# Two mixers' ends by token tiles, latent columns as 352 and 352, and a state product moved ahead of a level

## The reference

```python
def second_block(x, ...):
    for l in range(2):
        h = _rmsnorm(x, mix_norm[l])
        c_q, c_kv, k_pe, hq, hf, hi, hg = jnp.split(h @ w_in[l], splits, axis=-1)   # 384, 256, 64, 4 x 512
        a = _mla(c_q, c_kv, k_pe, positions, ...)            # 4 heads, causal
        r = _hgrn2(hq, hf, hi, hg, lower[l], hg_out_norm[l]) # 4 heads
        x = x + jnp.concatenate([a, r], axis=-1) @ w_out[l]
        x = x + (_swiglu if l == 0 else _moe)(_rmsnorm(x, ffn_norm[l]), ...)
    return _rmsnorm(x, final_norm)

def _mla(...):
    q = (_rmsnorm(c_q, q_a_norm) @ w_q_b)      # per head 128 + 64 columns, the 64 are rotated
    kv = (_rmsnorm(c_kv, kv_a_norm) @ w_kv_b)  # per head 128 of keys, 128 of values
    ...                                        # softmax over the keys up to the query, times v

def _hgrn2(q_raw, f_raw, i_in, g_raw, lower_bound, out_norm):
    q = silu(q_raw); f = lb + (1 - lb) * sigmoid(f_raw)
    log_f = log(f); k = (1 - lb) * sigmoid(-f_raw)
    S_t = diag(f_t) S_{t-1} + (1 - f_t) outer i_t; o_t = S_t^T q_t
    return _rmsnorm(o, out_norm) * silu(g_raw)
```

## Time and profile before

| | us |
|---|---|
| median of 3 runs | 1884.51 |
| lowest and highest | 1883.92, 1885.49 |
| the profiled execution | 1884.52 |
| its span in the profile | 1882.6 |
| PE busy in the span | 1859.7 (99%) |
| DVE busy | 1520.7 (81%) |
| ACT busy | 1240.1 (66%) |
| POOL busy | 402.8 (21%) |

### The profile page before, as it was taken

How to read it: one execution, slowest core, us unless ns; L and a number is a source line. 1 busy time by engine, 2 the same in 40 slices (tenths; PEclk the granted TensorE clock), 3 DMA queues, 4 the chain that set the end, 5 groups by cost and what they waited for, 6 DMA issues and landing times.

```text
span 1882.6 us, 26088 instructions
## 1 busy us (share of the span) xinstructions
PE 1859.7 (99%) x9336; PEld 1563.7 (83%) x9336; DVE 1520.7 (81%) x1650; ACT 1240.1 (66%) x1484; POOL 402.8 (21%) x206
## 2 busy tenths in 40 slices
PE   9999999999999999999999999999999999999997
PEld 7888889888888888878888888888888888888886
DVE  6745357777776887697699999999999999999997
ACT  6654444444754344565588888888888888888876
POOL 6856870002734000371630000000000000000000
PEclk9999999999999999999999999999999999999999
DMA  9534556665444666534699999999999999999994
GB/s 287 169 123 135 179 179 226 223 232 179 132 138 134 218 238 224 163 125 146 221 381 396 391 383 376 388 395 366 388 367 390 395 364 389 366 387 395 371 396 184
DMA packets 251542, 524.20 MB, mean 278 GB/s; under 512 B 9960, under 2 KB 58736, under 8 KB 251328
## 3 DMA queue, kind: packets, MB, share of 16 engines
q1 hardware_dynamic: 243408, 504.00, 74.7%
q10 hardware_dynamic: 5824, 12.06, 1.8%
q0 software_dynamic: 2224, 7.01, 1.2%
HBM read 507.71 MB, written 15.34 MB: 278 GB/s over the span
## 4 chain that ended last, share of the span: by engine, by line
PE 90%; DVE 7%; ACT 1%; issue 1%; DMA 1%; POOL 0%; SPq 0%; DVEq 0%; ACTq 0%
PE bank L740 24%; PE bank L742 24%; PE bank L741 24%; PE bank L1101 6%; PE bank L1104 3%; PE bank L863 1%; PE bank L1368 1%; PE bank L836 1%; DVE arena L1950 1%; DVE arena L2441 1%; DVE arena L1954 1%; PE bank L1182 1%; DMA arena<-in_w_in 1%; DVE arena L2106 1%; PE bank L842 0%
## 5 line engine op out<-in xcount | busy, mean ns | idle before, releaser
L1999 DVE TENSOR_TENSOR w_lo_sb<-arena,w_hi_sb 128x1024 fp32r<-128x1024 f32 x672 | 807.7, 1223 | 74.0 <-ACT w_hi_sb L1522 43.8
L1522 ACT ACTIVATE w_hi_sb<-arena 128x1024 fp32r<-128x1024 f32 x672 | 711.2, 1062 | 168.6 <-PE bank L742 167.9
L740 PE MATMUL bank<-w_hi_sb,left_sb 128*128 128x512 f32 (+1 forms) x1400 | 553.2, 395 | 1.4 <-POOL w_lo_sb L669 1.3
L742 PE MATMUL bank<-w_hi_sb,left_sb 128*128 128x512 f32 (+1 forms) x1400 | 542.2, 387 | 0.0
L741 PE MATMUL bank<-w_lo_sb,left_sb 128*128 128x512 f32 (+1 forms) x1400 | 541.5, 387 | 0.0
L1542 ACT ACTIVATE w_hi_sb<-arena 128x1024 fp32r<-128x1024 f32 (+1 forms) x269 | 278.2, 1051 | 300.8 <-PE bank L742 218.6
L669 POOL TENSOR_TENSOR w_lo_sb<-arena,w_hi_sb 128x1024 fp32r<-128x1024 f32 (+1 forms) x134 | 341.1, 2564 | 536.9 <-ACT w_hi_sb L1542 473.9
L740 PEld LDWEIGHTS bank<-w_hi_sb,left_sb 128*128 128x128 f32 x1400 | 263.1, 188 | 57.9 <-POOL w_lo_sb L669 3.5
L742 PEld LDWEIGHTS bank<-w_hi_sb,left_sb 128*128 128x128 f32 x1400 | 262.9, 188 | 54.9
L741 PEld LDWEIGHTS bank<-w_lo_sb,left_sb 128*128 128x128 f32 x1400 | 263.4, 188 | 50.9 <-issue 0.7
L740 PE MATMUL bank<-w_hi_sb,hid_hi_sb 128*128 128x512 f32 x656 | 257.3, 392 | 0.1
(11 more groups left out here) (365 smaller groups left out, 1676.1 us busy)
## 6 DMA issues: line engine op xcount, KB each, us to landing
arena<-in_moe_w_gate SPq DMA_DIRECT2D x112, 1024.0 KB, 7.6
arena<-in_moe_w_up SPq DMA_DIRECT2D x112, 1024.0 KB, 8.0
arena<-in_moe_w_down SPq DMA_DIRECT2D x112, 1024.0 KB, 7.8
arena<-in_w_in SPq DMA_DIRECT2D x45, 1024.0 KB, 5.1
arena<-in_w_ffn_in SPq DMA_DIRECT2D x22, 1024.0 KB, 5.1
arena<-in_w_out SPq DMA_DIRECT2D x12, 1024.0 KB, 5.0
arena<-in_w_ffn_out SPq DMA_DIRECT2D x11, 1024.0 KB, 4.8
arena<-in_dense_w_gate SPq DMA_DIRECT2D x11, 1024.0 KB, 5.4
```

Source lines behind the costliest of these rows:

```text
L740: pe.matmul(out, still[0], moving[0], start=start, stop=False)
L742: return pe.matmul(out, still[1], moving[0], start=False, stop=stop)
L1522: act.activation(expert_buffer(w_hi_sb, j), expert_piece(j % MOE_SUBS), ACT.Copy) \
L1999: dve.tensor_tensor(expert_buffer(w_lo_sb, j), expert_piece(j % MOE_SUBS), expert_buffer(w_hi_sb, j).bitcast(F32), ALU.subtract) \
```

## The change

It has seven parts.

1. The latents are c0 and c1 of 352 columns each, loaded as two loads of four k tiles each, so that both have four pieces of two k tiles.
2. PE makes level 2 behind the fourth piece of c1 (before: the second of two) and level 3 behind the second piece of hi (before: the first).
3. In layer 1 the logarithm of the bounds' rest is taken earlier on ACT, and DVE makes the keys' logarithm as two sums, of which the first needs the bounds alone.
4. The reciprocal root of the latents' mean squares is ACT's Sqrt and DVE's reciprocal instead of ACT's Ln and Exp; the means (`mean_c`) are taken ahead of level 2.
5. PE makes the state product ahead of level 5, between the two key/value products; DVE copies it right behind its taking of level 4.
6. The mixer's end goes by token tiles: transposes of the weights, products with the values, transposes of the mixed rows and the rounding for tile 0, then for tile 1. The outputs of the linear attention go through the gemm banks and are copied by ACT. `first_mixed` takes the first two weight pieces, tile by tile, and makes the transposes of tile 1 in between.
7. `finish_bounds` is cut into four steps, at units 3 to 6 of f2.

The diff, cut to its core:

```diff
+C_HALF = (Q_RANK + KV_RANK + ROPE) // 2
...
-        add(f"c0_{layer}", w, 0, 512)
-        add(f"c1_{layer}", w, 512, base - 512)
+        add(f"c0_{layer}", w, 0, base // 2)
+        add(f"c1_{layer}", w, base // 2, base // 2)
...
-                 (f"hqT_{layer}", 2), *level[0:4], (f"cT_{layer}", 3), *level[4:6], (f"hst_{layer}", 1),
+                 (f"hqT_{layer}", 2), *level[0:4], (f"cT_{layer}", 3), level[4], (f"hst_{layer}", 1), level[5],
                  (f"mpT_{layer}", 2), level[6], (f"msc0_{layer}", 2),
-                 level[7], (f"msc1_{layer}", 2), (f"ho_{layer}", 2), (f"mP_{layer}", 3), (f"mo_{layer}", 2),
-                 (f"mixT_{layer}", 4),
+                 level[7], (f"msc1_{layer}", 2), (f"mP0_{layer}", 1), (f"mo0_{layer}", 1), (f"mP1_{layer}", 2),
+                 (f"mixA_{layer}", 1), (f"mo1_{layer}", 1), (f"mixB_{layer}", 3),
...
-                gemm(f"c1_{l}", between={1: lambda: level(2)})
-                gemm(f"hi_{l}", between={0: lambda: level(3), 2: turn_c})
+                gemm(f"c1_{l}", between={3: lambda: level(2)})
+                gemm(f"hi_{l}", between={1: lambda: level(3), 2: turn_c})
...
+                for t in range(T):
+                    job = gemm_at[f"wo0_{layer}"] + t
+                    b, tokens = gemm_bank[job % 4][:, :], slice(t * P, (t + 1) * P)
+                    pe.wait_ge(sem("gemm_read"), job - 3)
+                    pe.wait_ge(sem("mix_hi_ready"), layer * T + t + 1)
+                    for j in range(2):
+                        pe.wait_ge(sem(lo_count[first + j][0]), lo_count[first + j][1])
+                        for k in range(2):
+                            for w in (w_hi[j], w_lo[j]):
+                                pe.matmul(b, hi_left[:, 2 * j + k, tokens], w[:, k, :],
+                                          start=(j == 0 and k == 0 and w is w_hi[0]), stop=False)
+                    if t == 0:
+                        turn_tile(1)
+                    pe.wait_ge(sem("pair_read"), read[t])
+                    for j in range(2):
+                        for k in range(2):
+                            mm = pe.matmul(b, lo_left[:, 2 * j + k, tokens], w_hi[j][:, k, :], start=False, stop=False)
...
                 for i in range(2):
                     head_gemm(f"kvb{i}_{l}", Q_RANK // P)
                     if i == 0:
+                        pe.wait_ge(sem("n_kt_ready"), l + 1)
+                        b = pair(f"hst_{l}", 0)
...
                         level(5)
...
+                turn_weights(0)
...
+                attend(0)
+                turn_weights(1)
+                turn_tile(0)
+                attend(1)
...
-                link(act.activation(head_rinv[:, 8:12], head_ms[:, 8:12], ACT.Ln))
-                act.activation(head_rinv[:, 8:12], head_rinv[:, 8:12], ACT.Exp, scale=-0.5) \
-                    .then_inc(sem("c_rinv"), 1)
+                act.activation(head_rinv[:, 8:12], head_ms[:, 8:12], ACT.Sqrt).then_inc(sem("c_rinv"), 1)
...
+                for t in range(T):
+                    act.wait_ge(sem("ho_full"), l * T + t + 1)
+                    act.activation(n_o[:, t, :], gemm_bank[(gemm_at[f"ho_{l}"] + t) % 4][:, :], ACT.Copy) \
+                        .then_inc(sem("gemm_read"), 1)
...
-                    if tag == "f2" and u == 3:
-                        finish_bounds()
+                    if tag == "f2" and 3 <= u < 7:
+                        finish_bounds(u - 3)
...
+                    dve.wait_ge(sem("rest_log"), 1)
+                    link(dve.scalar_tensor_tensor(n_k, n_z, 0.0, over(log_rest, 1, T), ALU.max, ALU.subtract))
...
+                    dve.tensor_tensor(n_k, n_k, soft, ALU.add).then_inc(sem("n_k_ready"), 1)
...
                 level_take(4)
+                copy_out(f"hst_{l}", 0, n_st)
                 level_scale(5)
                 level_diff(6)
...
                 level_take(5)
                 level_diff(7)
-                copy_out(f"hst_{l}", 0, n_st)
...
+                copy_out(f"mP0_{l}", 0, n_pT[0].rearrange("p h b q -> p (h b q)"))
+                own_share(0)
+                for i in range(2):
+                    copy_out(f"mP1_{l}", i, n_pT[1][:, 2 * i:2 * i + 2, :, :].rearrange("p h b q -> p (h b q)"))
+                dve.wait_ge(sem("w_used"), span[f"hi_{l}"][1])
+                split_tile(0)
+                own_share(1)
...
+                split_tile(1)
                 gate_hgrn()
```

184 lines of the change are left out of this document (90 added, 94 removed).

## The result

The changed kernel takes 1892.95 us (median of 6 runs, 1889.36 to 1894.58) where the kernel before takes 1885.15 us beside it (1883.92 to 1886.2): a ratio of 1.0038, with a 95% interval of 1.0026 to 1.0051. That is 7.8 us slower. The forecast was 1884.4 us and no change, with a range up to 1889.0; both failed, and the time lies outside the range.

The account below looks back on a forecast made before the run. The tensor engine, busy 99% of the span, was taken to bound the kernel. From 1884.52 us, terms of -1.9 + 0.3 - 2.5 - 1.0 + 7.7 - 2.7 = -0.1 us gave 1884.4 us, range 1880.6 to 1889.0.

Parts of the forecast that it names:

- The state product: Mixer, ahead of level 5: DVE's early copy holds up its queue, so PE waits 1.7 and 3.0 us; +3.85 us a layer.
- The matmul of 352 columns: Latents: equal columns of 352 start 0.159 us apart, saving 0.94 us a layer, -1.9 us in all.
- The 0.3 us that layer 0 was to give back: Layer 0, level 0: PE arrives earlier after a shorter piece and waits for DVE's copies; +0.3 us.
- The tile-wise end: Mixer's end, from the scores to the first output block: fewer waits when done by tiles; -1.35 us a layer, -2.7 us.
- The bounds: Dense feed-forward: DVE's work on the bounds' reciprocals, cut into steps, no longer delays a weight piece; -1.0 us.
- the waits of layer 1: Layer 1: waits for the keys and level 3 go, gate sum's stays, latents' turn is early enough; -2.5 us.
- The gate sum ahead of it keeps its wait: Layer 1, gate sum ahead of the keys: wait unchanged, as f and its logarithm stay on its path.
- With one load, and the mean taken ahead of level 2, it is early enough: Turn of the latents: one ACT table load instead of two at 1.28 us each, so it is not late.
- The wait for level 3: Layer 1: level 3 behind the values' second piece, 2.7 us later, so its 1.2 us wait goes.
- the chance given to the clock: Rival: PE's 3.0 us pause lowers the clock behind the scores, 2.8 to 5.7 us a layer, 1890 to 1896; 9%.
- the text's own signs of being wrong: Wait ahead of scores under 1.5 us, clock below full behind it, or PE waiting for POOL inside the latents.
- the rival on POOL's pieces: Rival, latents: POOL's shorter pieces still take 2.3 us, so PE waits 0.7 to 2.6 us; 1886 to 1889.6, 14%.

Follow-up runs that it names:

- experiment 1: The changed kernel with the state product and its copy back in their old places: 1881.68 us, ratio 0.9982 to the kernel before.
- experiment 2: The kernel before with only the state product moved ahead of level 5 and its copy right behind level 4's taking: 1895.41 us, ratio 1.0057.
- experiment 9: Changed kernel with layer 1's logarithms in the old order and the state's copy moved behind the queries' rotation, product still early: 1879.09 us.
- experiment 7: Changed kernel with state product, its copy, layer 1's logarithms and the mixer's end all as before the change: 1882.59 us, against 1879.68 with the tile-wise end.
- experiment 12: The kernel of experiment 10 with all four steps of the bounds at unit 3 of f2: 1879.12 us, against 1878.0.
- experiment 3: The changed kernel with layer 1's logarithms and the keys' sum back in the old order: 1889.4 us, ratio 1.0024 to the kernel before.
- experiment 5: The kernel before with only the latents' columns changed to 352 and 352: 1889.86 us, ratio 1.0022.
- experiment 6: The kernel of experiment 5 with the latents' two small mean operations moved from DVE into ACT's squares and logarithm: 1882.15 us, ratio 0.9984.
- experiment 10: The kernel of experiment 9 with the latents' means moved from DVE into ACT's squares and square root: 1878.0 us, ratio 0.9963.
- experiment 8: Changed kernel with state product and copy in old places and DVE's old keys' order, keeping only ACT's early logarithm in layer 1: 1880.0 us, ratio 0.9974.
- experiment 11: The kernel of experiment 10 plus layer 1's two keys' sums, with ACT's logarithm right behind its residual squares: 1880.37 us, ratio 0.9973.

## Why the prediction was wrong

**Right were four terms, among them the largest.**
- The state product: +3.85 us a layer forecast, +3.8 measured, with waits of 1.6 and 2.7 us for the 1.7 and 3.0 of the text. Experiments 1 and 2 show it as the cause and experiment 9 that it is the copy's place in DVE's order, as the text derived from the order alone.
- The matmul of 352 columns: 0.159 us forecast. The first and the last of 21 matmuls in a row of c1 start (518.20 - 515.02) / 20 = 0.159 us apart:

```profile
515.02 0.32 PE L744 MATMUL bank<-w_hi_sb,left_sb 128*128 128x352 f32 x1
...
518.20 0.32 PE L746 MATMUL bank<-w_hi_sb,left_sb 128*128 128x352 f32 x1
```

  Over the whole stretch it is 0.161, and -1.0 us a layer for the -0.94 of the text. The 0.3 us that layer 0 was to give back did not come.
- The tile-wise end: -1.35 us a layer forecast, -1.3 in the trace, and -2.9 us in all by experiment 7 for the -2.7.
- The bounds: -1.0 us forecast, -1.3 in the trace, -1.1 by experiment 12.

**Wrong was the term "the waits of layer 1", in what it says of the gate sum and of the turn of the latents.** It was -2.5 us and came out at +4.2 by the table: 2.5 + 1.4 for the gate sum and the keys, 1.0 - 0.7 for the values and the turn of the latents, with the clock.
- "The gate sum ahead of it keeps its wait, because f and its logarithm are on its path as before." They are not: the first sum stands ahead of them on DVE, and the early logarithm stands ahead of weight pieces on ACT, which brings POOL's row beside DVE's chain. The wait went from 0.5 to 2.9 us, and the low clock behind it cost 2.8 more. The step looked at which operation the transposes wait for, and not at what had been put ahead of the gate on both engines; and it gave the first sum no duration, which beside POOL is 3.3 us. Experiment 3 gives back 3.6 us. That the keys' own wait of 1.3 us goes was right.
- "With one load, and the mean taken ahead of level 2, it is early enough." It waits 0.7 us in both layers, where it did not wait before. The mean did not come earlier at all, since it needs ACT's squares, and those end at 522.9 us in both kernels. It only took longer, beside POOL, and held up the taking of level 2, which now stands behind it. First before, then after:

```profile
522.98 0.37 DVE L1958 TENSOR_SCALAR small_sb<-small_sb 128x2 f32<-128x2 f32 x2 [0.97 <-ACT arena L1774]
```

```profile
522.99 2.67 DVE L1982 TENSOR_SCALAR small_sb<-small_sb 128x2 f32<-128x2 f32 x2 [4.31 <-ACT arena L1796]
```

  Experiments 5 and 6, which differ in nothing but who does the work of these two operations, lie 7.7 us apart, more than the two waits of 4.5 us: in layer 1 the clock fell behind the wait as well, for some 1.7 us.
- The wait for level 3 did go, as forecast.

**Wrong was the chance given to the clock.** The rival had 9% with a price of 2.8 to 5.7 us a layer. The mechanism was right and its chance too small, and the price too high: 1.6 us a layer behind the scores, since the clock is low for some 3 us there and not for all of the 5.65. It also came at a third place, the gate sum, which the text did not have as a pause at all. Without it the changed kernel's profiled run would be 6.0 us shorter: 1.6 + 1.6 + 2.8. That the measured 1892.95 us lies inside this rival's 1890 to 1896 is in part luck: the clock behind the scores makes 3.2 us of it, the stretch around the gate sum, which the rival does not have, makes the rest. One of the text's own signs of being wrong, a clock below full behind the scores, did come.

**Half right was the rival on POOL's pieces.** Alone a piece of 704 words takes 1.71 us, beside DVE's work 1.93 on average, and over all sixteen of the changed kernel 1.81, as taken (1.8). The condition of this rival, 2.3 us a piece, did not come. But c1's four pieces, which were two, run into those of hi, and the row without a gap ends 2.8 us later than before, at 525.6 us. PE did not wait for POOL, as the rival said, but for DVE behind POOL; and the price was that of a tiny operation, which the text did not cost at all, as "one load less" was all it saw there.

**What stays open.** Why the clock falls behind one pause of 2.7 us and not behind another of equal length. In three profiled runs it fell behind four of six such pauses ahead of the scores (both layers of the changed kernel, layer 1 in experiment 2, layer 0 in experiment 3), and the low stretch began at once or 1.9 to 2.0 us later. The runs' spread fits it, and so does the chance wait of 0.9 us told under 10, but no experiment here took the two apart. The square root in place of logarithm and exponential (part 4) was not run alone.

## What to carry to other kernels

When a producer is moved earlier on one engine, leave the consumer on an in-order engine where its input is certain to be there: everything queued behind it pays for the wait, here 10 to 11 us for a copy of 0.7. Anything put ahead of the critical chain on any engine it passes, be it an idle-looking slot, has to be costed at its duration beside POOL's work, and a tiny operation is no exception. Ask too what it pushes later: an early logarithm on ACT moved POOL's pieces beside operations that had been free of them. Price a pause of TensorE of the lengths that brought the low clock here (2.4 to 3.0 us, seven of nine) with the slow stretch behind it.

## What the runs showed of the hardware

- A DVE operation on 128 by 2 numbers took 2.33 us beside POOL's pieces and about 0.19 without; it started 0.1 us behind a piece and ended with it. Which of the two comes first decides: at one place, 0.01 to 0.02 us between their starts made 2.38 us of 0.17 (experiment 10). The Trainium skill, "SBUF — State Buffer", section on the two separate sides, has the loser of the shared port pair wait for the whole instruction; this trace agrees, and shows that the size of the loser does not matter.
- After pauses of 2.7 us the granted clock fell in some places and in others not (four of six), in programs that differ elsewhere or in the other layer of the same one. It fell behind both pauses of 2.9 to 3.0 us ahead of the gate sum (after, experiment 1). It did not fall behind the 1.6 us ahead of level 5, nor behind waits of 1.7 us (experiment 8), 2.0 us (experiment 11) and 2.1 us (experiment 5, layer 0), where the granted clock of the next stretch was 1.00. In the columns' kernel (experiment 5) a wait of 2.4 us in layer 1 was followed by ten matmuls that held PE for 855.02 - 852.98 = 2.04 us, where they took 1.07 before (851.31 to 852.38):

```profile
852.98 2.39 PE L863 MATMUL bank<-const_sb,arena 128*128 128x128 f32 x10 [2.43 <-DVE arena L2493]
```

  The Trainium skill, "TensorE: Matmul & The Clock Gate", section on the HAM clock gate, has the clock follow how busy the array has been; the rows agree in kind.
